# Two more slabs of each DeltaNet group as seven half-size block products, with their sums on VectorE inside the triangular inverse

## The chip, the cores and the metric

The kernel runs on one core of a Trainium2 chip, in one launch. The metric is the device time of the launch in microseconds. TensorE multiplies, VectorE and ScalarE do the elementwise work, GpSimd helps a little, and SyncE's queue issues all loads. Everything is float32.

## The reference

One transformer layer for 256 tokens of width 2048. A token mixer multiplies x by `w_in`, and its columns feed three things: an S5 branch (2048 columns, called u), a DeltaNet branch (q and k with 16 heads, v and z with 32 heads, 128 wide each), and two gates. The branches are merged and multiplied by `w_mix_out`. After a layer norm come 32 routed experts and a second layer norm. What matters here is the DeltaNet branch, cut to its core:

```python
qkv = silu(causal_depthwise_conv(qkv, conv_w))
q, k = l2_normalize(q), l2_normalize(k)
# per head and chunk: a unit lower triangular system
lower = tril(kb @ k.T * decay, -1) + eye
sol = triangular_solve(lower, [v * beta, kb * exp(g)])
# the chunks follow each other through the state S
v_new = u_chunk - w_chunk @ S
o = q_dec @ S + attn_intra @ v_new
S = S * g_last + k_dec.T @ v_new
# the output of the branch
o = o * rsqrt(mean(o * o) + eps) * norm_w * silu(z)
```

z enters only in the last line, as `silu(z)`.

## The kernel before, in words

**Stages.** A short prologue transposes x and computes the decay gates. Then come eight DeltaNet groups of four value heads and two key heads each, to about 911 us. Then the eight u slabs and the S5 scan, the output products of both branches with the gates, `w_mix_out`, and from about 1840 us on the experts, during which the loads run without a pause.

**Slabs.** A group needs six slabs of 256 columns of `w_in`, numbered r = 0 to 5: q, k, v, v, z, z. A slab is 2 MB and is loaded by SyncE's queue into `ring[r % 3]` (`load_slot`, line 347). Each load waits until the slab before it in that ring place has been used by TensorE (`bank_ready[r % 3]`).

**Slabs 0 to 3** are computed by `seven_heads` (line 689). A slab and x are each cut into 2 by 2 blocks, and the four output blocks are made of seven block products instead of eight (Strassen's scheme in Winograd's form). That is 7 x 8 = 56 products of 128 x 128 weights with 128 columns. Four of the seven need sums of blocks of x (made once, `dn_xsum`), and three need sums of blocks of the weights, which VectorE makes for each slab with four additions of 128 x 1024 numbers (`sums_one`, `sums_two`, `sums_three`, lines 1698 to 1714, into `dn_wsum[r % 2]`; one is written over the slab itself). TensorE waits for them (`prepared`) only ahead of product 16, because the first two block products use plain blocks. The seven results lie in two banks of PSUM (`dn_first`, `dn_second`), and `join_heads` (line 1770) adds them up on VectorE with five instructions.

**Slabs 4 and 5 (z)** are computed by `part` (line 668) as 32 plain products of 128 x 128 weights with 256 columns each, into bank 1 (`z0`) and bank 2 (`z1`). ScalarE takes each with one `Silu` from the bank into `zs` (lines 1434 to 1443).

Every product written in the program is two MATMUL records in the trace, so the 64 products of two z slabs are 128 records, and the 56 of another slab are 112.

**Order of a group on TensorE, written out by hand** (`group`, from line 733): the column sums for the l2 norm; slab 3; small products for the decay; `z0(0, 19)`; transposes of v; and then the inverse. Between all of these, z products serve to fill the time in which TensorE would wait for another engine.

**The inverse.** The triangular inverse runs in six levels over half blocks for both chunks c = 0, 1, and a seventh step that joins the halves. One level goes back and forth between two engines:

- TensorE forms the first products of chunk 0 and chunk 1 (line 800) and then runs `z0(19 + 2 * lv, 21 + 2 * lv)`, two z products.
- VectorE masks each result (line 1844, `Pm`).
- TensorE forms the second products of both chunks (lines 811 and 818) and then runs `z1(lv, lv + 1)`, one z product.
- VectorE subtracts them from the inverse (line 1852, called the update here). Then the next level's line 800 may run, chunk by chunk (`t_ready[c]`).

The seventh step is lines 831 and 840 with `z0(31, 32)`, `z1(8, 9)` and `z1(9, 11)` beside it.

**The chunks.** After the inverse come the products of the state (lines 849 to 874) with the remaining 21 z products of `z1` between them, each waiting for VectorE or ScalarE (`apply_dve`, `apply_act`). ScalarE squares the outputs, VectorE reduces the squares (line 1896), ScalarE takes logarithm and exponential, and VectorE scales the outputs (line 1901, `otok`). `front` (line 727) then computes slabs 0 to 2 of the next group, with `turn_outputs` (line 680), the transposes of the outputs, after slab 0. The last multiplication with `zs` is line 1910.

**SyncE's queue at the end of the groups** (line 379 on): the load of u slab 0; small loads for S5 (`lam_re`, `lam_im`, `log_dt`, four loads of `b_re` and `b_im` in runs of 64 bytes, `d_skip`); the loads of u slabs 1 and 2, which wait for `z0` and `z1` of the last group.

Of the kernel before, what the change touches and what calls it, by code (L numbers as in the profile page):

```python
# [67 lines left out]
DN_PREPARED = 1 + 4 * GROUPS  # L68
# [4 lines left out]
def build(nc, x, w_in, conv_w, a_log, dt_bias, norm_w, w_dn, lam_re, lam_im, log_dt, b_re, b_im, c_re, c_im,  # L73
# [3 lines left out]
    with ExitStack() as ctx:  # L77
# [93 lines left out]
        dn_first, dn_second = (0, 5, 1, 0), (1, 6, 2, 7)  # L171
# [173 lines left out]
        def _(sp):  # L345
# [33 lines left out]
            load_slot(S_U % RING, in_rows(w_in[:, 0:SC]), 0, U_USE)  # L379
            sp.dma_start(spar[0:NJ, 0, :], lam_re.rearrange("(j g) n -> j (g n)", g=2)).then_inc(s5_lam_loaded, 16)  # L380
# [7 lines left out]
            for r in range(1, 3):  # L388
                load_slot((S_U + r) % RING, in_rows(w_in[:, SC * r:SC * r + SC]), r, U_USE)
# [257 lines left out]
        def _(pe):  # L647
# [31 lines left out]

            def turn_outputs(g):  # L680

                pe.wait_ge(apply_dve, 4 * g + 4)
                for a in range(GV):
                    for c in range(2):
                        col = (a % 2) * T + c * P
                        last = tr(ps[3 + a // 2][:, col:col + P], otok[:, c, a], ident[:, :])
                last.then_inc(apply_pe, 1)

            def seven_heads(g, r, lo, hi):
# [3 lines left out]
                if lo == 0:  # L693
# [4 lines left out]
                    if r == 2:  # L698
                        pe.wait_ge(bank_taken[0], 2 * g + 2)
                        pe.wait_ge(bank_taken[1], 2 * g + 1)  # L700
                    if r == 3:
                        pe.wait_ge(kd_in, 1)

# [13 lines left out]
                for i in range(lo, hi):  # L717
                    if i == KD:
                        pe.wait_ge(prepared, 4 * g + 2 + r)
# [13 lines left out]
            def group(g, more):  # L733
# [26 lines left out]
                def z0(lo, hi):  # L760
                    part(16 * (2 * g + 2), 1, 1, 2 * g + 1, xT, lo, hi)

                def z1(lo, hi):
                    part(16 * (2 * g + 2), 2, 2, 2 * g + 1, xT, lo, hi)
# [5 lines left out]
                pe.wait_ge(bank_taken[2], 2 * g + 2)  # L770
                z0(0, 19)
# [19 lines left out]
                for lv in range(HALF_LEVELS):  # L791
# [11 lines left out]
                    z0(19 + 2 * lv, 21 + 2 * lv)  # L803
# [21 lines left out]
                    z1(lv, lv + 1 if whole else 8)  # L825
# [8 lines left out]
                z0(31, 2 * KD)  # L834
                z1(8, 9)
# [7 lines left out]
                z1(9, 11)  # L843
# [7 lines left out]
                z1(11, 15)  # L851
# [5 lines left out]
                for a in range(GV):  # L857
                    last = mm(ps[7][:, a * P:a * P + P], attn[:, 0, a], vn[:, 0, a], start=True, stop=True)
                last.then_inc(apply_pe, 1)
                z1(15, 18)  # L860
# [4 lines left out]
                z1(18, 24)  # L865
# [4 lines left out]
                z1(24, 28)  # L870
                pe.wait_ge(apply_dve, 4 * g + 3)
                for a in range(GV):
                    mm(ps[6][:, a * P:a * P + P], qd[:, a], Sst[:, a], start=True, stop=False)
                    last = mm(ps[6][:, a * P:a * P + P], attn[:, 1, a], vn[:, 1, a], start=False, stop=True)
                last.then_inc(apply_pe, 1)
                z1(28, 2 * KD)
# [3 lines left out]
                else:  # L880
                    part(16 * (2 * g + 3), 0, 0, 2 * g + 2, xT, 0, 4)
# [27 lines left out]
            part(16 * (2 * GROUPS + 1), 0, 0, U_USE, xT, 4, 26)  # L909
            turn_outputs(GROUPS - 1)  # L910
            part(16 * (2 * GROUPS + 1), 0, 0, U_USE, xT, 26, 2 * KD)
# [464 lines left out]
        def _(act):  # L1376
# [22 lines left out]
            with act.Fori(0, GROUPS) as g:  # L1399
# [34 lines left out]
                act.wait_ge(bank_ready[1], 2 * g + 2)  # L1434
                A(zs[:, 0:2], ps[1][:, :].rearrange("p (h t) -> p h t", h=2), ACT.Silu).then_inc(bank_taken[1], 1)
# [3 lines left out]
                A(sq[:, 0:512], ps[7][:, :], ACT.Square)  # L1439
                act.wait_ge(apply_pe, 7 * g + 6)  # L1440
                A(sq[:, 512:1024], ps[6][:, :], ACT.Square).then_inc(osq_ready, 1)
                act.wait_ge(bank_ready[2], 2 * g + 2)
                A(zs[:, 2:4], ps[2][:, :].rearrange("p (h t) -> p h t", h=2), ACT.Silu).then_inc(bank_taken[2], 1)
# [10 lines left out]
            def take_u(r):  # L1454
                act.wait_ge(bank_ready[r % 3], U_USE + r // 3 + 1)
                nc.scalar.copy(uT[:, 2 * r:2 * r + 2, :],
                               ps[r % 3][:, :].rearrange("p (k t) -> p k t", k=2)).then_inc(bank_taken[r % 3], 1)
# [220 lines left out]
        def _(dve):  # L1678
# [19 lines left out]
            def sums_one(g, r):  # L1698
# [4 lines left out]
                dve.drain()  # L1703
                V.tensor_tensor(ring[:, buf, 0:8, P:SC], ring[:, buf, 0:8, 0:P], ring[:, buf, 0:8, P:SC], ALU.subtract)

# [46 lines left out]
            def dn_group(g, more):  # L1752
# [17 lines left out]
                def join_heads(r):  # L1770

                    at_ = [4 * dn_first[r] + i for i in range(4)] + [4 * dn_second[r] + i for i in range(3)]
# [10 lines left out]
                    V.tensor_tensor(at(w0, 2, 512)[:, :, 0:P], twice(dn_partial[:, 3]), two(1, 2), ALU.add)  # L1783
# [3 lines left out]
                    V.tensor_tensor(dn_joined.rearrange("p (a n) -> p a n", a=2)[:, :, P:2 * P], twice(dn_partial[:, 2]),  # L1787
                                    two(4, 5), ALU.add)
                    V.tensor_tensor(dn_joined[:, 2 * P:3 * P], dn_partial[:, 1], regions[:, at_[3]], ALU.add)
# [3 lines left out]
                def decay(c):  # L1793

                    dve.wait_ge(gb_ready, 2 * g + c + 1)
                    for a in range(GV):
# [15 lines left out]
                                ALU.mult).then_inc(qk_ready, 1)  # L1812
                dve.wait_ge(tok_ready, 2 * g + 1)
                V.tensor_copy(ktok, ps[5][:, 0:GQ * P].rearrange("p (b d) -> p b d", b=GQ)).then_inc(tok_taken, 1)
                decay(0)
                join_heads(3)
# [24 lines left out]
                for lv in range(HALF_LEVELS):  # L1841
                    for c in range(2):
# [4 lines left out]
                                        ALU.mult).then_inc(pm_ready[c], 1)  # L1847
                    for c in range(2):
# [25 lines left out]
                def by_head(v, width):  # L1874
# [4 lines left out]
                                by_head(beta[:, 0, ds(GV * g, GV)], P), ALU.mult).then_inc(apply_dve, 1)  # L1879
                if more:  # L1880
# [13 lines left out]

                dve.wait_ge(osq_ready, g + 1)
# [4 lines left out]
                for c in range(2):  # L1900
                    V.tensor_tensor(otok[:, c], ps[7 - c][:, :].rearrange("p (a d) -> p a d", a=GV),
# [5 lines left out]
                dve.wait_ge(bank_taken[2], 2 * g + 3)  # L1907
# [556 lines left out]
```

## Time and profile before

| | us |
|---|---|
| median of 3 runs | 2832.26 (2831.66 to 2834.74) |
| the profiled execution, time | 2834.3 |
| the profiled execution, span | 2832.6 |
| TensorE busy | 2775.6 (98% of the span) |
| VectorE busy | 1252.3 (44%) |
| ScalarE busy | 446.0 (16%) |
| one group, slab 3 to slab 3 (617.04 to 728.22) | 111.18 |

Times in the trace count from the start of the span. "Idle before" stands in brackets behind a row, with what ended it. A TensorE record's duration overlaps with the next record's, so the pace of a row of products is read from start to start, not from the mean duration.

### The profile page before, as it was taken

The numbers are of one execution on the slowest core, as the hardware profiler recorded it, in microseconds if no ns is written. First come the engines' busy times: TensorE is split into PE (matmuls) and PEld (weight loads), VectorE is DVE, ScalarE is ACT, GpSimd is POOL, SyncE is SP. The second block draws the span as 40 slices with busy tenths as digits, with TensorE's granted clock in tenths as the row PEclk, the third lists the DMA queues.
The fourth block names the chain that finished last, engine by engine and source line by source line (L and its number), as shares of the span: only waits on it lengthen the run. The fifth ranks groups of instructions, "written<-read, shape, count | busy, mean of one in ns | idle before, by whom it ended". The sixth has DMA issues, their size and how long they took to land.

```text
span 2832.6 us, 53479 instructions
## 1 busy us (share of the span) xinstructions
PE 2775.6 (98%) x22343; PEld 2072.8 (73%) x22343; DVE 1252.3 (44%) x2593; ACT 446.0 (16%) x773; POOL 63.7 (2%) x115
## 2 busy tenths in 40 slices
PE   8999999999999999999999999999999999999997
PEld 8899898898898888888899999843444444444442
DVE  6566565665664327777665652221111211112114
ACT  3121121221221111110010000131112111112110
POOL 1000000000000000000000000000000000000000
PEclk9999999999999999999999999999999999999999
DMA  7233242343344523444477556378999999999997
GB/s 218 88 122 120 90 149 91 107 142 98 102 149 107 163 90 123 130 136 137 145 210 228 178 161 226 149 293 362 422 422 422 422 422 422 422 422 422 422 422 280
DMA packets 328854, 654.12 MB, mean 231 GB/s; under 512 B 45232, under 2 KB 274736, under 8 KB 279536
## 3 DMA queue, kind: packets, MB, share of 16 engines
q1 hardware_dynamic: 328688, 651.61, 62.7%
q8 instruction: 141, 2.31, 0.3%
q14 instruction: 25, 0.20, 0.0%
HBM read 649.49 MB, written 2.10 MB: 230 GB/s over the span
## 4 chain that ended last, share of the span: by engine, by line
PE 88%; DMA 7%; DVE 2%; DVEq 2%; issue 1%; ACT 0%; SPq 0%; ACTq 0%
PE bank L723 14%; PE bank L675 14%; PE bank L1054 10%; PE bank L1244 9%; PE bank L975 8%; PE bank L1282 7%; DMA arena<-in_w_up_dram 7%; PE bank L1223 4%; PE bank L1109 4%; PE bank L1322 4%; PE bank L800 1%; PE bank L818 1%; PE bank L938 1%; PE bank L811 1%; PE bank L1254 1%
## 5 line engine op out<-in xcount | busy, mean ns | idle before, releaser
L675 PE MATMUL bank<-arena 128*128 128x256 f32 x2048 | 484.8, 386 | 0.0
L1244 PE MATMUL bank<-arena 128*64 128x512 f32 x2048 | 445.5, 594 | 12.3 <-DMA arena<-in_w_up_dram 12.3
L675 PEld LDWEIGHTS bank<-arena 128*128 128x128 f32 x2048 | 374.9, 190 | 52.3
L723 PEld LDWEIGHTS bank<-arena 128*128 128x128 f32 x3584 | 403.9, 192 | 4.2 <-issue 3.8
L723 PE MATMUL bank<-arena 128*128 128x128 f32 x3584 | 405.5, 275 | 0.0
L1244 PEld LDWEIGHTS bank<-arena 128*64 128x64 f32 x2048 | 144.5, 137 | 311.3 <-issue 281.5
L1054 PEld LDWEIGHTS bank<-arena 128*128 128x128 f32 x2576 | 287.8, 192 | 0.1
L1054 PE MATMUL bank<-arena 128*128 128x128 f32 x2576 | 287.8, 275 | 0.0
L975 PE MATMUL bank<-arena 128*128 128x256 f32 x1024 | 223.5, 380 | 0.0
L2356 DVE TENSOR_SCALAR arena<-bank 128x512 f32<-128x512 f32 x16 | 11.1, 691 | 465.8 <-PE bank L1244 465.8
L975 PEld LDWEIGHTS bank<-arena 128*128 128x128 f32 x1024 | 194.0, 190 | 26.7
L1282 PE MATMUL bank<-arena 128*64 128x512 f32 x960 | 211.0, 598 | 0.5 <-ACT arena L1631 0.5
L1282 PEld LDWEIGHTS bank<-arena 128*64 128x64 f32 x960 | 67.7, 138 | 133.1 <-issue 132.4
L1621 ACT ACTIVATE arena<-bank,small 128x128 f32<-128x128 f32 x256 | 96.3, 456 | 232.0 <-PE bank L1223 232.0
L2383 DVE TENSOR_TENSOR arena<-arena,bank 128x512 f32<-128x512 f32 x120 | 82.4, 687 | 105.2 <-PE bank L1322 105.0
L1223 PEld LDWEIGHTS bank<-arena 128*128 128x128 f32 x1024 | 118.4, 196 | 12.4 <-issue 11.4
L2012 DVE TENSOR_TENSOR arena<-arena 128x256 f32<-128x256 f32 x256 | 109.3, 427 | 32.5 <-issue 15.5
L1223 PE MATMUL bank<-arena 128*128 128x128 f32 x1024 | 121.4, 281 | 0.9 <-ACTq L1577 0.9
L1109 PE MATMUL bank<-arena 128*128 128x256 f32 x512 | 114.0, 381 | 0.0
L1322 PE MATMUL bank<-arena,masks 128*128 128x512 f32 x240 | 109.8, 596 | 1.8 <-DVEq L2370 1.8
L1109 PEld LDWEIGHTS bank<-arena 128*128 128x128 f32 x512 | 96.1, 190 | 12.4
L2365 DVE TENSOR_SCALAR arena<-bank 128x512 f32<-128x512 f32 x16 | 11.1, 691 | 206.8 <-PE bank L1244 206.8
(341 smaller groups left out, 2412.8 us busy)
## 6 DMA issues: line engine op xcount, KB each, us to landing
arena<-in_w_in_dram SPq DMA_DIRECT2D x72, 2048.0 KB, 8.7
arena<-in_w_up_dram SPq DMA_DIRECT2D x64, 2048.0 KB, 16.5
arena<-in_w_gate_dram SPq DMA_DIRECT2D x64, 2048.0 KB, 13.9
arena<-in_w_down_dram SPq DMA_DIRECT2D x64, 2048.0 KB, 21.1
arena<-in_w_dn_out_dram SPq DMA_DIRECT2D x16, 2048.0 KB, 8.2
arena<-in_w_glu_b_dram SPq DMA_DIRECT2D x8, 2048.0 KB, 8.2
arena<-in_w_glu_a_dram SPq DMA_DIRECT2D x8, 2048.0 KB, 8.2
arena<-in_w_mix_out_dram SPq DMA_DIRECT2D x8, 2048.0 KB, 14.3
```

Source lines behind the costliest of these rows:

```text
L675: last = mm(ps[bank][:, ct * T:ct * T + T], ring[:, buf, k, ct * P:ct * P + P], rhs[:, k, :], start=k == 0, stop=k == KD - 1)
L723: last = mm(regions[:, 4 * bank + place % 4], left(k), right(k), start=k == 0, stop=k == KD // 2 - 1)
L975: last = mm(ps[bank][:, ct * T:ct * T + T], ring[:, n % 2, k, ct * P:ct * P + P], oT[:, half * KD + k, :], start=half == 0 and ct == 0 and ...
L1054: last = mm(banks[:, base + P * place:base + P * place + P], left(k), right(k), start=k == 0, stop=k == KD // 2 - 1)
L1109: last = mm(ps[bank][:, 0:SC], mg[:, k, m * P:m * P + P], mixw[r][:, k, :], start=k == 0, stop=k == KD - 1)
L1223: last = mm(ps[4 + b][:, k * P:k * P + P], h1[:, m, 4 * b + k], Psel[:, m].rearrange("p o c -> p (o c)"), start=m == 0, stop=m == MT - 1)
L1244: last = mm(ps[bank][CAP * o:CAP * o + CAP, :], xg[:, 4 * q + k, CAP * o:CAP * o + CAP], w[:, o, k], start=False, stop=q == 3 and k == 3, ...
L1282: last = mm(ps[4 + n][CAP * o:CAP * o + CAP, :], shT[:, k, CAP * o:CAP * o + CAP], buf[:, o, n * 512:n * 512 + 512], start=k == 0, stop=k ...
L1322: last = mm(ps[bank][:, :], pwT[:, (n // 4) * P:(n // 4) * P + P], ysb[:, (n % 4) * 512:(n % 4) * 512 + 512], start=not biased, stop=True, ...
L1621: last = A(xg[:, k, :], ps[4 + b][:, P * j:P * j + P], ACT.Identity, scale=gqk[:, k:k + 1], bias=bqk[:, k:k + 1])
L2012: V.tensor_tensor(prod, prev.unsqueeze(2).to_broadcast([P, 2, 2, NJ]), rot, ALU.mult)
L2383: V.tensor_tensor(av, av, ps[(2, 3, 0, 1)[n % 4]][:, :], ALU.add).then_inc(sc_taken, 1)
```

## The change

- Slabs 4 and 5 are computed by `seven_heads` too: 56 products with 128 columns each in place of 32 with 256 columns. Slab 4 uses banks 1 and 2, slab 5 banks 0 and 7. Slab 0 moves from banks 0 and 1 to 1 and 2.
- Their weight sums are new on VectorE: those of slab 4 around the copy of `ktok` and `decay(0)`, those of slab 5 one addition each in levels 0 to 3 of the inverse, between the two masks and the two updates.
- Their results are joined by `join_heads(4)` after the first `vn`, and `join_heads(5)` ahead of the reduction of the squares, into `zs`. ScalarE's two `Silu` read and write `zs` in SBUF and come after these joins.
- The z products are dealt out anew over the group. In level 0, four of them stand between the first products of chunk 0 and those of chunk 1.
- The outputs of the chunks go to banks 6 and 4 in place of 7 and 6. The first u slab goes to bank 5.
- At the end of the groups, u slab 1 is loaded ahead of the small S5 loads, and these wait for the end of the last `z1`; u slab 2 is loaded after them.

```diff
-DN_PREPARED = 1 + 4 * GROUPS
+DN_PREPARED = 1 + 6 * GROUPS
...
-        dn_first, dn_second = (0, 5, 1, 0), (1, 6, 2, 7)
+        dn_first, dn_second = (1, 5, 1, 0, 1, 0), (2, 6, 2, 7, 2, 7)
...
             load_slot(S_U % RING, in_rows(w_in[:, 0:SC]), 0, U_USE)
+            load_slot((S_U + 1) % RING, in_rows(w_in[:, SC:2 * SC]), 1, U_USE)
+            sp.wait_ge(bank_ready[2], U_USE)
             sp.dma_start(spar[0:NJ, 0, :], lam_re.rearrange("(j g) n -> j (g n)", g=2)).then_inc(s5_lam_loaded, 16)
             sp.dma_start(spar[0:NJ, 1, :], lam_im.rearrange("(j g) n -> j (g n)", g=2)).then_inc(s5_lam_loaded, 16)
             sp.dma_start(coef[0:NJ, 15, 0:2], log_dt.rearrange("(j g) -> j g", g=2)).then_inc(s5_lam_loaded, 16)
...
             sp.dma_start(dsk, d_skip.rearrange("(k a) q -> (a q) k", k=KD), allow_slow_non_contiguous=True).then_inc(s5_loaded, 16)
-            for r in range(1, 3):
-                load_slot((S_U + r) % RING, in_rows(w_in[:, SC * r:SC * r + SC]), r, U_USE)
+            load_slot((S_U + 2) % RING, in_rows(w_in[:, 2 * SC:3 * SC]), 2, U_USE)
...
+            def first_u(lo, hi):
+                if lo == 0:
+                    pe.wait_ge(slot_loaded[0], 16 * (2 * GROUPS + 1))
+                    pe.wait_ge(bank_taken[0], U_USE + 1)
+                for i in range(lo, hi):
+                    ct, k = divmod(i, KD)
+                    last = mm(ps[5][:, ct * T:ct * T + T], ring[:, 0, k, ct * P:ct * P + P], xT[:, k, :],
+                              start=k == 0, stop=k == KD - 1)
+                if hi == 2 * KD:
+                    last.then_inc(bank_ready[0], 1)
...
                     if r == 2:
                         pe.wait_ge(bank_taken[0], 2 * g + 2)
-                        pe.wait_ge(bank_taken[1], 2 * g + 1)
                     if r == 3:
+                        pe.wait_ge(bank_taken[2], 2 * g + 1)
                         pe.wait_ge(kd_in, 1)
+                    if r == 4:
+                        pe.wait_ge(bank_taken[2], 2 * g + 2)
+                    if r == 5:
+                        pe.wait_ge(vtok_taken, g + 1)
...
-                        pe.wait_ge(prepared, 4 * g + 2 + r)
+                        pe.wait_ge(prepared, 6 * g + 2 + r)
...
                 def z0(lo, hi):
-                    part(16 * (2 * g + 2), 1, 1, 2 * g + 1, xT, lo, hi)
+                    seven_heads(g, 4, lo, hi)
                 def z1(lo, hi):
-                    part(16 * (2 * g + 2), 2, 2, 2 * g + 1, xT, lo, hi)
+                    seven_heads(g, 5, lo, hi)
...
-                pe.wait_ge(bank_taken[2], 2 * g + 2)
-                z0(0, 19)
+                z0(0, 37)
...
-                    z0(19 + 2 * lv, 21 + 2 * lv)
+                        if lv == 0 and c == 0:
+                            z0(37, 41)
+                    if lv > 0:
+                        z0(39 + 2 * lv, 41 + 2 * lv)
...
-                    z1(lv, lv + 1 if whole else 8)
+                    z1(2 * lv, 2 * lv + 2 if whole else 16)
...
-                z0(31, 2 * KD)
-                z1(8, 9)
+                z0(51, 54)
...
-                z1(9, 11)
+                z0(54, 56)
+                z1(16, 18)
...
-                z1(11, 15)
+                z1(18, 26)
...
-                    last = mm(ps[7][:, a * P:a * P + P], attn[:, 0, a], vn[:, 0, a], start=True, stop=True)
+                    last = mm(ps[6][:, a * P:a * P + P], attn[:, 0, a], vn[:, 0, a], start=True, stop=True)
...
-                z1(15, 18)
+                z1(26, 32)
...
-                z1(18, 24)
+                z1(32, 43)
...
-                z1(24, 28)
+                z1(43, 50)
...
-                    mm(ps[6][:, a * P:a * P + P], qd[:, a], Sst[:, a], start=True, stop=False)
-                    last = mm(ps[6][:, a * P:a * P + P], attn[:, 1, a], vn[:, 1, a], start=False, stop=True)
+                    mm(ps[4][:, a * P:a * P + P], qd[:, a], Sst[:, a], start=True, stop=False)
...
-                z1(28, 2 * KD)
+                z1(50, 56)
...
-                    part(16 * (2 * g + 3), 0, 0, 2 * g + 2, xT, 0, 4)
+                    first_u(0, 4)
...
-            part(16 * (2 * GROUPS + 1), 0, 0, U_USE, xT, 4, 26)
+            first_u(4, 26)
             turn_outputs(GROUPS - 1)
-            part(16 * (2 * GROUPS + 1), 0, 0, U_USE, xT, 26, 2 * KD)
+            first_u(26, 2 * KD)
...
-                act.wait_ge(bank_ready[1], 2 * g + 2)
-                A(zs[:, 0:2], ps[1][:, :].rearrange("p (h t) -> p h t", h=2), ACT.Silu).then_inc(bank_taken[1], 1)
                 act.wait_ge(apply_pe, 7 * g + 2)
                 nc.scalar.copy(Sst, ps[4][:, :].rearrange("p (a d) -> p a d", a=GV)).then_inc(apply_act, 1)
                 act.wait_ge(apply_pe, 7 * g + 3)
-                A(sq[:, 0:512], ps[7][:, :], ACT.Square)
+                A(sq[:, 0:512], ps[6][:, :], ACT.Square)
+                act.wait_ge(bank_taken[1], 2 * g + 3)
+                A(zs[:, 0:2], zs[:, 0:2], ACT.Silu)
                 act.wait_ge(apply_pe, 7 * g + 6)
-                A(sq[:, 512:1024], ps[6][:, :], ACT.Square).then_inc(osq_ready, 1)
-                act.wait_ge(bank_ready[2], 2 * g + 2)
-                A(zs[:, 2:4], ps[2][:, :].rearrange("p (h t) -> p h t", h=2), ACT.Silu).then_inc(bank_taken[2], 1)
+                A(sq[:, 512:1024], ps[4][:, :], ACT.Square).then_inc(osq_ready, 1)
+                act.wait_ge(bank_taken[2], 2 * g + 3)
+                A(zs[:, 2:4], zs[:, 2:4], ACT.Silu)
...
-                               ps[r % 3][:, :].rearrange("p (k t) -> p k t", k=2)).then_inc(bank_taken[r % 3], 1)
+                               ps[r % 3 if r else 5][:, :].rearrange("p (k t) -> p k t", k=2)).then_inc(bank_taken[r % 3], 1)
...
-            def sums_one(g, r):
+            def sum_first(g, r):
 
                 buf = r % RING
                 dve.wait_ge(slot_loaded[buf], 16 * (2 * g + r // 3 + 1))
                 V.tensor_tensor(dn_wsum[r % 2][:, 0], ring[:, buf, 0:8, P:SC], ring[:, buf, 8:16, P:SC], ALU.add)
                 dve.drain()
+
+            def sum_own(g, r):
+                buf = r % RING
                 V.tensor_tensor(ring[:, buf, 0:8, P:SC], ring[:, buf, 0:8, 0:P], ring[:, buf, 0:8, P:SC], ALU.subtract)
+
+            def sums_one(g, r):
+                sum_first(g, r)
+                sum_own(g, r)
...
+                    to_off = w0 if r < 4 else SH + 8960 + 512 * (r - 4)
+                    to = dn_joined if r < 4 else at(to_off, 512)
+                    reach = w0 + 512 - to_off
...
-                    V.tensor_tensor(dn_joined.rearrange("p (a n) -> p a n", a=2)[:, :, P:2 * P], twice(dn_partial[:, 2]),
+                    V.tensor_tensor(to.rearrange("p (a n) -> p a n", a=2)[:, :, P:2 * P], twice(dn_partial[:, 2]),
                                     two(4, 5), ALU.add)
-                    V.tensor_tensor(dn_joined[:, 2 * P:3 * P], dn_partial[:, 1], regions[:, at_[3]], ALU.add)
+                    V.tensor_tensor(to[:, 2 * P:3 * P], dn_partial[:, 1], regions[:, at_[3]], ALU.add)
...
+                sums_one(g, 4)
+                sums_two(g, 4)
                 dve.wait_ge(tok_ready, 2 * g + 1)
                 V.tensor_copy(ktok, ps[5][:, 0:GQ * P].rearrange("p (b d) -> p b d", b=GQ)).then_inc(tok_taken, 1)
                 decay(0)
+                sums_three(g, 4)
                 join_heads(3)
...
+                    if lv == 0:
+                        sum_first(g, 5)
+                    if lv == 1:
+                        sum_own(g, 5)
+                    if lv == 2:
+                        sums_two(g, 5)
+                    if lv == 3:
+                        sums_three(g, 5)
...
+                join_heads(4)
                 if more:
                     sums_one(g + 1, 0)
...
+                join_heads(5)
...
-                    V.tensor_tensor(otok[:, c], ps[7 - c][:, :].rearrange("p (a d) -> p a d", a=GV),
+                    V.tensor_tensor(otok[:, c], ps[6 - 2 * c][:, :].rearrange("p (a d) -> p a d", a=GV),
...
-                dve.wait_ge(bank_taken[2], 2 * g + 3)
```

## Rows read from the trace of the kernel before

**Rows 1.** The page, parts 1 and 4: busy time by engine, and the chain that ended last.
```profile
PE 2775.6 (98%) x22343; PEld 2072.8 (73%) x22343; DVE 1252.3 (44%) x2593; ACT 446.0 (16%) x773; POOL 63.7 (2%) x115
...
PE 88%; DMA 7%; DVE 2%; DVEq 2%; issue 1%; ACT 0%; SPq 0%; ACTq 0%
```

**Rows 2.** Timeline of TensorE: start, us, engine, line, operation, tiles, count; one front stage.
```profile
133.88 12.67 PE L723 MATMUL bank<-arena 128*128 128x128 f32 x112
...
146.39 1.04 PE L686 MATMUL bank<-ident,arena 128*128 128x128 f32 x8
```

**Rows 3.** Timeline of TensorE, last group's end and the u slabs.
```profile
940.50 41.71 PE L675 MATMUL bank<-arena 128*128 128x256 f32 x192
982.04 3.66 PE L906 MATMUL bank<-ident,arena 128*128 128x128 f32 x32
```

**Rows 4.** Timeline of VectorE, group 0: one slab's sums and a join.
```profile
56.40 1.22 DVE L1702 TENSOR_TENSOR arena<-arena 128x1024 f32<-128x1024 f32 x1 [0.19 <-issue]
...
57.70 1.23 DVE L1704 TENSOR_TENSOR arena<-arena 128x1024 f32<-128x1024 f32 x1
...
58.84 1.22 DVE L1707 TENSOR_TENSOR arena<-arena 128x1024 f32<-128x1024 f32 x1
...
61.47 0.29 DVE L1781 COPY arena<-bank 128x128 f32<-128x128 f32 x1
...
63.78 0.61 DVE L1758 TENSOR_SCALAR arena<-arena,cw 128x256 f32<-128x256 f32 x2 [0.33 <-issue]
```

**Rows 5.** Timeline of VectorE, group 6 to 7: before and at the fourth slab's join.
```profile
734.67 1.23 DVE L1811 TENSOR_TENSOR arena<-arena 128x1024 f32<-128x1024 f32 x1 [0.19 <-issue]
...
744.20 0.29 DVE L1781 COPY arena<-bank 128x128 f32<-128x128 f32 x1 [4.12 <-PE bank L723]
```

**Rows 6.** Timeline, group 0: entry of the inverse.
```profile
87.99 0.68 DVE L1826 TENSOR_TENSOR arena<-bank,arena 128x512 f32<-128x512 f32 x1
...
88.84 0.46 PE L800 MATMUL bank<-arena 64*64 64x64 f32 x16 [1.21 <-DVEq L1830]
```

**Rows 7.** Timeline, group 0: one level of the inverse (level 3).
```profile
100.83 0.93 PE L800 MATMUL bank<-arena 64*64 64x64 f32 x32
101.36 0.88 DVE L1844 TENSOR_TENSOR arena<-bank,arena 128x256 f32<-128x256 f32 x2 [0.24 <-PE bank L800]
...
101.69 1.13 PE L675 MATMUL bank<-arena 128*128 128x256 f32 x4
...
102.75 0.46 PE L811 MATMUL bank<-arena 64*64 64x64 f32 x16
...
103.72 1.50 DVE L1852 TENSOR_TENSOR arena<-arena,bank 128x512 f32<-128x512 f32 x2 [1.48 <-PE bank L818]
...
104.29 0.70 PE L675 MATMUL bank<-arena 128*128 128x256 f32 x2
...
104.92 0.93 PE L800 MATMUL bank<-arena 64*64 64x64 f32 x32
```

**Rows 8.** Timeline, group 0: end of the inverse and the first products of the chunks.
```profile
114.89 0.65 PE L831 MATMUL bank<-arena 64*64 64x64 f32 x8 [0.19 <-DVEq L1863]
...
118.56 1.05 PE L849 MATMUL bank<-arena 128*128 128x128 f32 x8
```

**Rows 9.** Timeline, group 0: the root of the output norm on VectorE and ScalarE.
```profile
132.98 1.22 DVE L1896 TENSOR_REDUCE small<-arena 128x8 f32<-128x1024 f32 x1 [2.32 <-ACT arena L1441]
...
137.91 1.29 DVE L1901 TENSOR_TENSOR arena<-bank,small 128x512 f32<-128x512 f32 x2 [3.71 <-ACTq L1448]
```

**Rows 10.** Timeline of SyncE's queue at the end of the groups.
```profile
855.99 1.72 SPq L380 DMA_DIRECT2D arena<-in_s_lam_re_dram  x1
...
872.75 3.01 SPq L387 DMA_DIRECT2D small<-in_s_d_dram  x1
...
911.84 0.56 SPq L351 DMA_DIRECT2D arena<-in_w_in_dram  x1
```

**Rows 11.** Windows: TensorE, its loads, VectorE, ScalarE, GpSimd, clock, DMA share, GB/s.
```profile
919.00:922.00 3.00, 3.00 (x16) 2.64 (x15) 0.00 (x0) 0.00 (x0) 0.00 (x0) 1.00 0.28 85
```

More of the change, by code:

```diff
@@ L869, in group @@
                 last.then_inc(apply_pe, 1)
-                z1(24, 28)
+                z1(43, 50)
                 pe.wait_ge(apply_dve, 4 * g + 3)
                 for a in range(GV):
-                    mm(ps[6][:, a * P:a * P + P], qd[:, a], Sst[:, a], start=True, stop=False)
-                    last = mm(ps[6][:, a * P:a * P + P], attn[:, 1, a], vn[:, 1, a], start=False, stop=True)
+                    mm(ps[4][:, a * P:a * P + P], qd[:, a], Sst[:, a], start=True, stop=False)
+                    last = mm(ps[4][:, a * P:a * P + P], attn[:, 1, a], vn[:, 1, a], start=False, stop=True)
                 last.then_inc(apply_pe, 1)
-                z1(28, 2 * KD)
+                z1(50, 56)
                 if more:
@@ L1782, in join_heads @@
                     dve.drain()
-                    V.tensor_tensor(at(w0, 2, 512)[:, :, 0:P], twice(dn_partial[:, 3]), two(1, 2), ALU.add)
+                    V.tensor_tensor(at(to_off, 2, reach)[:, :, 0:P], twice(dn_partial[:, 3]), two(1, 2), ALU.add)
                     dve.drain()
```

## The prediction

> **What bounds the kernel now.** I read the page's busy times and its chain first. TensorE is busy for 98% of the span and holds 88% of the chain that ended last; VectorE is at 44% [rows 1]. So time falls only where TensorE has less to do, or waits less. The loads run without a pause only in the experts, behind everything changed here; their first loads wait for TensorE's earlier products, so what a group saves should reach the end whole.
>
> Next, the pace of the two kinds of product, from start to start. A stretch of 112 records with 128 columns takes 146.39 - 133.88 = 12.51 us, 0.1117 us a record [rows 2]. A stretch of 192 records with 256 columns takes 41.54 us, 0.2164 us a record [rows 3]. Half the columns cost 0.516 of the time.
>
> Last, the timeline of one group, since the new sums land where TensorE and VectorE hand work back and forth. Two things are to be seen there. VectorE has a pause of 1.48 us in each level, ahead of its updates [rows 7]. And at the entry TensorE already waits 1.21 us for VectorE [rows 6].
>
> **The change part by part**, for one group.
>
> *TensorE's work.* Two slabs: 128 records x 0.2164 = 27.70 us go, 224 x 0.1117 = 25.02 us come: -2.68 us. That is the gain if no wait changes. The walk below asks which do.
>
> *Entry of the inverse.* TensorE's start on chunk 1 in level 0 is set by VectorE: its work ends at 87.99 + 0.68 = 88.67, and TensorE starts at 88.84, 0.17 us later [rows 6]. That chain of VectorE begins at the join of slab 3, which waits 4.12 us for TensorE [rows 5]. The sums of slab 4 go in ahead of it. An addition followed by a drain occupies 1.30 us, one without 1.14 us [rows 4]; the first three take 1.30 + 1.14 + 1.30 = 3.74 us and the fourth 1.30. From 735.90, with about 0.5 us for the copy of `ktok` and 1.3 us for `decay(0)`, VectorE is done at about 742.8; the join starts at 744.20 [rows 5]. So they cost nothing, covered by that wait of 4.12 us, with 1.4 us to spare; without that cover they would cost 5.0 us less the pause. TensorE's own way there changes by 74 x 0.1117 - 38 x 0.2164 = +0.04 us, and the four z products before chunk 1 (0.89 us, 1.1 with the change of tile size) fit into the idle 1.21 us. Change: 0.
>
> *Levels 0 to 3.* I follow chunk 1, from its first products in one level to those in the next. Before: from 88.84 [rows 6] to 104.92 + 0.43 = 105.35 [rows 7], taking half of the pair's 0.86 for chunk 0, 16.51 us for four levels, 4.13 us each. TensorE's own path now: first products 0.86, z part 1.06 - 0.42 = 0.64 (two half-size products for two whole), second products 1.54, z part 0.65, in all 3.69 us. VectorE's path: 0.53 us from TensorE's start to the mask (100.83 to 101.36), 0.44 for the mask, 1.30 for the new addition, 0.81 to the second update, 0.69 for it, 0.17 back to TensorE [rows 4, 6, 7] = 3.94 us. It is the longer one, because the pause of 1.48 us shrinks by the 0.42 us of z work taken out, to 1.06, and the addition does not quite fit. In level 1 the addition has no drain: 3.78 us. Four levels: 3 x 3.94 + 3.78 = 15.60 us, against 16.51: -0.91 us.
>
> *Level 4 to 5*, without an addition, is TensorE's again: 4.09 to 3.71 us (0.02 of it VectorE's): -0.38 us.
>
> *Level 5 to the first product of the chunks.* The z part of level 5 is 0.42 us shorter. The step on line 831 waits for VectorE as before [rows 8], so its time from the second products stays. The next z part is six records for four, -0.20 us; the last, eight for four, +0.03 us. Together -0.59 us.
>
> *The chunks.* 42 records x 0.2164 = 9.09 us become 76 x 0.1117 = 8.49 us: -0.60 us. `join_heads(4)` occupies VectorE for 63.78 - 0.33 - 61.47 = 2.0 us, 2.1 with its end [rows 4], and then come two sums; these 4.6 us fit between the first `vn` and the next result it must take, about 5.1 us later. It is tight, and if it misses by half a microsecond TensorE has about that much left before line 868.
>
> *The output norm.* `join_heads(5)` starts at the end of z and stands ahead of the reduction, which was at 132.98 [rows 9]. It ends some 2.1 us after that, so `otok` comes at about 139.2 instead of 137.91, and the sums for slab 1 end near 145.5. `turn_outputs` comes at 146.39 [rows 2], and the sums are needed 3.6 us after it. Cost 0. Slab 1's load starts some 2 us later, with over 10 us to spare.
>
> *End of the groups.* The S5 loads now stand between the end of `z1` and u slab 2. Before, that load was issued at 911.84. The chain of small loads took 855.99 to 872.75 + 3.01 = 19.8 us of the queue, u slab 2 needs some 8.4 us more (its transfer ended at about 920.2) [rows 10, 11], so it lands at +28.2 us. TensorE wants it at 940.50 [rows 3], +28.7 us. Cost 0, bounds 0 and 6: the 0.5 us could turn into a wait if the transfers are slower, but part of the 19.8 us was waiting behind a slab's transfer which is not there now.
>
> **Sum.** -0.91 - 0.38 - 0.59 - 0.60 = -2.48 us a group, 0.2 us less than TensorE's work alone says; eight groups: -19.8 us. The profiled execution took 2834.3 us (span 2832.6), 2.0 us above the median of 2832.26. Against it: 2814.5; against the median: **2812.4 us**.
>
> **Unknown prices.** No row shows an addition inside the pause. From below: it hides wholly and TensorE's 3.69 us rules; 15.60 becomes 14.76, 6.7 us better over all groups, 2805.7. From above: each addition stands in full on the old path, 4.09 - 0.42 + 1.30 = 4.97 us a level. I take 3.94, built from rows of this very loop.
>
> **Rivals.**
>
> *A, the addition takes the place of the work saved* (slower). Place: levels 0 to 3, between masks and updates. Price at 4.97 us a level: 4 x 4.97 - 15.60 = 4.28 us a group, +34.2 us on my sum: **2846.6 us**. It decides once a level takes over 3.90 + 19.8 / 32 = 4.52 us. For it: VectorE's path is the longer one. Against: the pause is a measured wait for TensorE, and the rows leave only 0.25 us uncovered.
>
> *B, the same place at half the price*: levels of about 4.2 us, because updates and masks also slip against each other. 32 x 0.3 = 9.6 us worse: **2822 us**.
>
> *C, u slab 2 comes late* by the bound of 6 us: **2818 us**. For it: a margin of 0.5 us by old issue times.
>
> *D, half-size products are bound by their weight load.* Each record loads 128 x 128 weights whether 128 or 256 columns follow. If a load's own 0.19 us (the recorded duration on line 723) were the pace, 224 x 0.19 = 42.6 us would stand against 27.7, +15 us a group: **2950 us** and slower. 
>
> **How the numbers follow.** My forecast 0.72, A 0.03, B 0.14, C 0.08, D 0.01; the last 0.02 for a saving that ends within the noise, such as late results in the chunks. A measurement of this kernel can tell about 0.2%, 5.7 us. Faster: 0.72 + 0.14 + 0.08 = 0.94; same 0.02; slower 0.04. The range goes from 2806 (additions hidden) to 2821 (most of B, and C).
>
> **What would show it.** Right: a group lasts 108.7 us instead of 111.2; the first products of chunk 1 follow each other by 3.8 to 4.0 us in levels 0 to 3 and by 3.7 into level 5, with short idle times of TensorE on line 800's successor that end on VectorE; no idle time at slab 3's join beyond the old; L1910's place unchanged against `turn_outputs`; no wait for a load near u slab 2. Wrong: levels of 4.2 us and more (B, A), VectorE's `R` late and TensorE idle ahead of line 868, or TensorE idle for a load after u slab 1 (C).

## The result, and the profile after

The changed kernel takes 2844.85 us (median of 6 runs, 2842.1 to 2847.0), the kernel before beside it 2832.9 us: a ratio of 1.0043, 95% interval 1.0032 to 1.0055. It is slower by 12 us where 20 us less were forecast. The profiled execution has a span of 2842.8 us.

The page of the changed kernel, parts 1, 3, 4 and 5 (compare [rows 1]):

```profile
PE 2763.6 (97%) x23111; PEld 2103.9 (74%) x23111; DVE 1353.1 (48%) x2737; ACT 446.0 (16%) x773; POOL 67.1 (2%) x115
...
q14 instruction: 55, 0.45, 0.0%
...
PE 70%; DVE 13%; DMA 8%; issue 4%; DVEq 4%; ACT 0%; SPq 0%; ACTq 0%
...
L739 PE MATMUL bank<-arena 128*128 128x128 f32 x5376 | 654.1, 280 | 19.4 <-DVEq L1737 19.3
```

TensorE is busy for 12.0 us less than before, and idle for 22.2 us more (79.2 in place of 57.0 us of the span). So the work did shrink, and waits ate the gain. A part of the gain in busy time went to a lower clock besides, as experiment 1 shows. VectorE now holds 13% of the chain, where it held 2%. Line 739 is the block product of `seven_heads`, and line 1737 is where VectorE reports a slab's sums done: 19.3 us of TensorE's waits stand there, and before there were none.

The waits of TensorE in the changed kernel from 61 to 855 us (waiter, releaser, us in all, times, longest):

```profile
PE bank L739 <- DVEq L1737: 19.3, 6, 3.5
PE bank L815 <- DVEq L1902: 6.6, 23, 0.4
```

and those of VectorE in it, from 0 to 950 us:

```profile
DVE arena L1809 <- PE bank L739: 38.8, 18, 4.0
DVE arena L1809 <- issue: 38.7, 8, 6.6
```

"issue" means that VectorE waited for nothing that the profile shows. Line 1809 is the first instruction of a join, and the first that counts as busy in the group's loop. Six of the eight are 6.1 to 6.6 us long, at the six jumps back of the loop (it runs seven times; the last group is written out behind it). In the kernel before, the waits on "issue" at the starts of groups 1 to 7 were 4.6 us in all. The timeline of VectorE in the changed kernel, where it goes from group 0 to group 1:

```profile
144.73 1.41 DVE L1950 SCALAR_TENSOR_TENSOR arena<-bank,small,arena 128x512 f32 x2 [1.26 <-PE bank L698]
152.40 0.29 DVE L1809 COPY arena<-bank 128x128 f32<-128x128 f32 x1 [6.26 <-issue]
```

and of TensorE there:

```profile
144.38 16.24 PE L739 MATMUL bank<-arena 128*128 128x128 f32 x144
163.80 10.82 PE L739 MATMUL bank<-arena 128*128 128x128 f32 x80 [3.17 <-DVEq L1737]
```

The bank that the join reads had been full since the transposes began at 143.51, so the 6.26 us are no wait for data. They put slab 2's sums late, and TensorE stands for 3.17 us in slab 2, ahead of product 16. Then its clock falls, as the windows of the changed kernel behind five of its waits show (the column before the last two is the granted clock):

```profile
165.00:168.00 3.00, 3.00 (x16) 3.00 (x16) 2.24 (x8) 0.00 (x0) 0.00 (x0) 0.50 0.03 10
390.50:396.50 6.00, 5.54 (x26) 5.54 (x27) 4.80 (x13) 0.00 (x0) 0.00 (x0) 0.50 0.33 105
506.50:509.00 2.50, 2.50 (x14) 2.50 (x14) 1.83 (x7) 0.00 (x0) 0.00 (x0) 0.50 0.25 76
619.00:625.00 6.00, 5.39 (x25) 5.39 (x26) 4.80 (x13) 0.00 (x0) 0.00 (x0) 0.50 0.32 101
735.00:738.00 3.00, 3.00 (x14) 3.00 (x15) 2.36 (x7) 0.00 (x0) 0.00 (x0) 0.50 0.33 103
```

0.50 is 1.2 GHz in place of 2.4. The five spells last some 24 us together. One of the six waits (3.45 us, up to 278.94) has none behind it, and in the groups of the kernel before there is none either.

What the forecast said of the other places held, in the main. Slab 3's join still waits for TensorE, 1.47 us now, where 1.4 were to be left (compare [rows 5]). The output norm came 0.8 us later than worked out: `otok` starts 6.4 us ahead of `turn_outputs`, where it was 8.5 us before and 7.2 were forecast (compare [rows 2, 9]). That cost nothing:

```profile
75.51 0.29 DVE L1809 COPY arena<-bank 128x128 f32<-128x128 f32 x1 [1.47 <-PE bank L739]
...
133.30 1.22 DVE L1937 TENSOR_REDUCE small<-arena 128x8 f32<-128x1024 f32 x1
137.09 1.29 DVE L1942 TENSOR_TENSOR arena<-bank,small 128x512 f32<-128x512 f32 x2 [2.57 <-ACTq L1466]
...
143.51 1.04 PE L698 MATMUL bank<-ident,arena 128*128 128x128 f32 x8
```

What VectorE waits for at the jump is told by the queues. DMA queues from 172 to 839 us, the kernel before:

```profile
q8 instruction: 62, 1.02, 0.6%
q14 instruction: 1, 0.01, 0.0%
```

and the changed kernel:

```profile
q8 instruction: 65, 1.06, 0.7%
q14 instruction: 27, 0.22, 0.1%
```

q14 brings instructions in packets of 8 KB. Before, one came in six groups; now 27 come, about five a group. And about the jump from group 0 to group 1, between 145 and 160 us of the changed kernel, three of them:

```profile
q14 instruction: 3, 0.02, 0.6%
```

In the traces of the kernel before and of experiment 1 no packet of q14 falls between 145 and 160 us. And between 146.5 and 152.2 us, while VectorE stands:

```profile
q1 hardware_dynamic: 1754, 1.78, 92.2%
q14 instruction: 1, 0.01, 0.4%
```

q1 is the load of a slab. The one packet of q14 starts some 4 us after the jump, and VectorE goes on 2 us later. Whether the packet waits behind the slab's load was not tested.

VectorE's loop over the groups went from 271 to 301 instructions (drains, register and semaphore instructions counted, which the page's counts leave out). By the Trainium skill ("Runtime: NRT & Kernel Launch", section "Instruction fetch mechanics") 16 KiB hold 256 instructions; an estimate from that figure is 128 for 8 KB. The trace of experiment 2 agrees: there VectorE's loop is written out, and a packet of q14 comes for every 128 of its instructions. From this came theory F, that the start of VectorE's loop is no longer held on the chip when it jumps back, and has to be brought again. Its rival, theory O, was that VectorE simply has too much to do. It is busy for about 100 us more over the kernel.

### The profile page after: what moved, and what is told of

Same layout as the page of the kernel before. It is cut to its first block, busy times and chain, and to the rows that moved or that the text cites. A ratio compares the mean times of both kernels' runs of the same rounds, so it can differ in the third digit from the quotient of the medians.

```text
span 2842.8 us, 55264 instructions
## 1 busy us (share of the span) xinstructions
PE 2763.6 (97%) x23111; PEld 2103.9 (74%) x23111; DVE 1353.1 (48%) x2737; ACT 446.0 (16%) x773; POOL 67.1 (2%) x115
## 4 chain that ended last, share of the span: by engine, by line
PE 70%; DVE 13%; DMA 8%; issue 4%; DVEq 4%; ACT 0%; SPq 0%; ACTq 0%
PE bank L739 18%; PE bank L1072 10%; PE bank L1262 8%; DMA arena<-in_w_up_dram 8%; PE bank L1300 7%; PE bank L1241 4%; PE bank L1127 4%; DVE arena L2052 4%; PE bank L1340 4%; PE bank L676 4%; DVE arena L2054 3%; DVE arena L2056 3%; PE bank L815 1%; PE bank L1272 1%; DVE arena L1891 1%
## 5 line engine op out<-in xcount | busy, mean ns | idle before, releaser
L739 PE MATMUL bank<-arena 128*128 128x128 f32 x5376 | 654.1, 280 | 19.4 <-DVEq L1737 19.3
L739 PEld LDWEIGHTS bank<-arena 128*128 128x128 f32 x5376 | 626.0, 194 | 32.0 <-DVEq L1737 20.4
L1072 PEld LDWEIGHTS bank<-arena 128*128 128x128 f32 x2576 | 287.8, 192 | 0.1
L1072 PE MATMUL bank<-arena 128*128 128x128 f32 x2576 | 287.8, 275 | 0.0
L993 PE MATMUL bank<-arena 128*128 128x256 f32 x1024 | 223.5, 380 | 0.0
L993 PEld LDWEIGHTS bank<-arena 128*128 128x128 f32 x1024 | 194.0, 190 | 26.7
L676 PE MATMUL bank<-arena 128*128 128x256 f32 x960 | 212.1, 381 | 0.0
L676 PEld LDWEIGHTS bank<-arena 128*128 128x128 f32 x960 | 181.1, 190 | 25.0
L1241 PEld LDWEIGHTS bank<-arena 128*128 128x128 f32 x1024 | 117.4, 194 | 12.0 <-issue 11.4
L1241 PE MATMUL bank<-arena 128*128 128x128 f32 x1024 | 120.4, 279 | 0.5 <-ACTq L1595 0.5
L1127 PE MATMUL bank<-arena 128*128 128x256 f32 x512 | 114.0, 381 | 0.0
L1127 PEld LDWEIGHTS bank<-arena 128*128 128x128 f32 x512 | 96.1, 190 | 12.4
```

The source lines that it names most:

```text
L676: last = mm(ps[bank][:, ct * T:ct * T + T], ring[:, buf, k, ct * P:ct * P + P], rhs[:, k, :], start=k == 0, stop=k == KD - 1)
L739: last = mm(regions[:, 4 * bank + place % 4], left(k), right(k), start=k == 0, stop=k == KD // 2 - 1)
L993: last = mm(ps[bank][:, ct * T:ct * T + T], ring[:, n % 2, k, ct * P:ct * P + P], oT[:, half * KD + k, :], start=half == 0 and ct == 0 and ...
L1072: last = mm(banks[:, base + P * place:base + P * place + P], left(k), right(k), start=k == 0, stop=k == KD // 2 - 1)
L1127: last = mm(ps[bank][:, 0:SC], mg[:, k, m * P:m * P + P], mixw[r][:, k, :], start=k == 0, stop=k == KD - 1)
L1241: last = mm(ps[4 + b][:, k * P:k * P + P], h1[:, m, 4 * b + k], Psel[:, m].rearrange("p o c -> p (o c)"), start=m == 0, stop=m == MT - 1)
```

## The experiments

In the profiles VectorE executes 48 instructions up to the loop's start in both kernels. The experiments move that start by drains in VectorE's prologue, where it waits about 5 us for ScalarE, and touch nothing in the loop:

```diff
+            for _ in range(N):
+                dve.drain()
             dve.wait_ge(sp_done, 1)
```

**1. The changed kernel, N = 40.**

> The changed kernel with 40 drains added on VectorE in the prologue, where it waits 5 us for ScalarE; nothing in the group loop is touched. Theory F (instruction fetch): VectorE's group loop has 301 instructions in place of 271 and now runs over one more 8 KB block (128 instructions) of its instruction stream, so that the block with the loop's start is gone at each jump back; VectorE stands 6.3 us there, TensorE then waits 3.2 us at slab 2's product 16, and its clock halves. Moved 40 instructions on, the loop lies within three blocks: no stall at the jump, no wait of TensorE there, about 2813 us (2809 to 2819). Rival O (overload): VectorE has 12 us more work a group and is late whatever the place of its code: 2843 to 2849 us, with the same 19 us of TensorE's waits.

2811.78 us (2811.32 to 2817.44), ratio 0.993 (0.9916 to 0.9943) to the kernel before. Forty instructions that do nothing make the changed kernel 33 us faster. TensorE is busy for 12.3 us less than without them:

```profile
PE 2751.3 (98%) x23111; PEld 2093.0 (74%) x23111; DVE 1353.4 (48%) x2737; ACT 446.0 (16%) x773; POOL 67.0 (2%) x115
```

VectorE at the same jump in this run:

```profile
144.08 1.41 DVE L1952 SCALAR_TENSOR_TENSOR arena<-bank,small,arena 128x512 f32 x2 [1.26 <-PE bank L698]
146.22 0.29 DVE L1811 COPY arena<-bank 128x128 f32<-128x128 f32 x1 [0.72 <-issue]
```

and TensorE, whose slabs 1 and 2 now run without a break:

```profile
143.74 25.18 PE L739 MATMUL bank<-arena 128*128 128x128 f32 x224
168.75 1.88 PE L752 MATMUL bank<-arena,ones 128*128 128x512 f32 x4
```

From 172 to 819 us no packet of q14 is left, and the clock stays at 2.4 GHz through all groups. VectorE's busy time is the same 1353 us, so theory O falls.

**2. The changed kernel with VectorE's loop written out.**

```diff
-            with dve.Fori(0, GROUPS - 1) as g:
+            for g in range(GROUPS - 1):
                 dn_group(g, True)
```

> The changed kernel with VectorE's group loop written out eight times, no jump back. Theory F: same as with the 40 drains, about 2813 us (2809 to 2820); the blocks are fetched in order ahead of their use. Rival O: 2843 to 2849 us. A third reading (fetching itself is slow, jump or no jump): stalls of microseconds spread over the groups, over 2830 us.

2816.77 us (2813.06 to 2817.51), ratio 0.9941 (0.9927 to 0.9955). No stall at what was the jump: VectorE is idle for 0.2 us there. With no loop, q14 shows the instructions going by. From 218.9 to 877.8 us:

```profile
q14 instruction: 12, 0.10, 0.0%
```

From the first of these packets to the last VectorE executes 1406 instructions, 127.8 from one to the next on the average (117 to 139). So q14 does bring VectorE's instructions, 128 in a packet.

A group takes 109.18 us against 108.64 in experiment 1 (from the first column sum of group 0 to that of group 7, divided by seven). Why it is some 5 us behind in all, 4 of them in the groups, is not settled; its waits on line 815 and a few of TensorE's own ("issue", up to 1.2 us each) are a little larger.

**3 and 4. The kernel before, N = 16 and N = 40.**

> The kernel before with 16 drains added in the same place of VectorE's prologue, loop body untouched (271 instructions). Theory F: its loop ends just ahead of a block boundary (no fetch was seen in it, and the changed loop fetches at its instruction 271); pushed 16 on, it crosses, and each of seven jumps costs VectorE about 6 us and TensorE about 2 to 3: 2846 to 2860 us. Boundary guessed within 17 instructions, so there is one chance in four that 16 misses it and the time stays at 2833. Rival O: 2833 us.

> The kernel before with 40 drains there. Theory F: the loop starts in the next block and ends before a boundary again: as before, 2831 to 2835 us. If drains in the prologue cost time in themselves, it shows here as some 2 us more. Rival O: 2833 us.

2831.19 us (2829.84 to 2833.05), ratio 0.9994 (0.9985 to 1.0003), and 2832.66 us (2831.37 to 2835.28), ratio 1.0 (0.9991 to 1.001). Drains there cost nothing. The forecast for 16, a stall and 2846 to 2860 us, missed. The run placed the boundary better, since its loop starts at instruction 64 and is held.

**5. The kernel before, N = 8.**

> The kernel before with 8 drains added in VectorE's prologue (16 and 40 of them left it at 2831 to 2833 us). From the fetches seen so far, blocks of VectorE's instructions begin near its 62nd to 66th, 190th and 318th to 322nd record; the loop before is records 48 to 318. Theory F: the loop is in reach when it lies within three blocks. With 16 drains it starts at 64, in the second block. With 8 it starts at 56, in the first, and ends at 326, in the fourth: the only place where the kernel before should stall. Then 5 fetches a group on the instruction queue, a stall of VectorE of about 5.5 us at each jump, about 3 us of TensorE's wait at slab 2's product 16 and spells at half clock: 2845 to 2865 us. If it stays at 2831 to 2835, the place of the loop against the blocks does not explain it and it was something else that the 40 drains moved in the changed kernel (its length of 301 against some limit that the drains can't have changed, so theory F would be short of a part).

2879.27 us (2877.06 to 2881.3), ratio 1.0167 (1.0151 to 1.0182). Eight instructions that do nothing make the kernel before 47 us slower, while 16 or 40 do nothing to it. The direction and the place are those of the forecast; the size is 14 us over its upper end. Of these, 12 us are TensorE's waits, 5 us each where 3 were expected. VectorE and TensorE at the first jump:

```profile
155.78 0.29 DVE L1783 COPY arena<-bank 128x128 f32<-128x128 f32 x1 [6.96 <-issue]
```

```profile
167.98 12.02 PE L723 MATMUL bank<-arena 128*128 128x128 f32 x80 [5.10 <-DVEq L1712]
```

and TensorE's waits for the sums from 61 to 900 us:

```profile
PE bank L723 <- DVEq L1712: 30.1, 6, 5.1
```

In the groups 34 us pass at 1.2 GHz, and TensorE is busy for 14.9 us longer (2790.5 us against 2775.6). With the 30.1 us of waits that is 45.0 us; the profiled executions differ by 44.6 us.

**6. The price of the four additions in the pause.** From experiment 1, without them:

```diff
                     if lv == 0:
-                        sum_first(g, 5)
+                        dve.wait_ge(slot_loaded[2], 16 * (2 * g + 2))
-                    if lv == 1:
-                        sum_own(g, 5)
-                    if lv == 2:
-                        sums_two(g, 5)
                     if lv == 3:
-                        sums_three(g, 5)
+                        dve.sem_inc(prepared, 1)
```

> The changed kernel with 40 drains in the prologue (2811.8 us), without the four additions for slab 5 that stand in levels 0 to 3 (slab 5's weight sums are left out, so that z is not the reference's). It measures their price in the pause, which the prediction put at 0.84 us a group, 6.7 us in all: TensorE's path of 3.69 us then rules the levels, 2805 us. Level by level the profile with the additions shows 3.84, 3.65, 3.87, 3.86 us and about 0.9 us of waits of TensorE a group: 2804 to 2807. If the additions were hidden after all: 2811 to 2812.

4729.19 us, a time that says nothing: with another z the tokens go to other experts, and the kernel takes its branch for experts with too many tokens. The groups come before that and can be read. From the column sums of group 0 to those of group 7 they take 815.2 - 60.1 us, 107.87 us each, against 108.64 us with the additions: 0.77 us a group, 0.84 forecast.

**7. Four products moved into the waits left in the inverse.** From experiment 1:

```diff
-                    z1(2 * lv, 2 * lv + 2 if whole else 16)
+                    z1(*((0, 4), (4, 6), (6, 9), (9, 12), (12, 14), (14, 20))[lv])
```

and the bounds of all later parts of `z1` four higher, the last being `z1(54, 56)`.

> The changed kernel with 40 drains in the prologue, and four of slab 5's products moved from behind the chunks' outputs into the waits that are left in the inverse: 4, 2, 3, 3, 2, 6 of them after the second products of levels 0 to 5 in place of 2, 2, 2, 2, 2, 6. All additions stay. The waits on line 815 add up to 7.6 us in the run it is made from; if they are filled: 2805 to 2808 us. If VectorE's path gets longer by what is put in (because the masks of the next level come later): 2811 to 2813 us.

2808.56 us (2804.4 to 2813.1), ratio 0.9919 (0.9905 to 0.9933). Its waits on line 815 in the groups:

```profile
PE bank L815 <- DVEq L1904: 2.7, 8, 0.3
```

down from 7.6 us. A group takes 107.70 us, 0.94 less than in experiment 1, where the waits had been 0.95. The median lies half a microsecond above the range that was expected. The two medians differ by 3 us with spreads of 6 and 9, so the gain shows in the groups' length more than in the total. This version has the lowest median of all that were run.

**8 and 9. The changed kernel, N = 16 and N = 112.**

> The changed kernel with 16 drains in place of 40. Theory F with the blocks as the runs so far place them (beginning near VectorE's record 62 to 64, 190, 318, 446): the loop of 301 records starts at 64 and ends at 364, three blocks: 2811 to 2815 us. If the first block ended later than at 64, the stall stays: 2843 to 2848 us.

> The changed kernel with 112 drains. By the same blocks the loop starts at record 160, in the second block, and ends at 460, in the fifth: it touches four blocks again, so the stall comes back although nothing was taken away: 2844 to 2852 us, of which up to 3 us are the drains themselves, that no longer all fit into VectorE's wait of 5 us. If any shift that is long enough helps: 2812 to 2816 us.

2814.73 us (2813.03 to 2816.62), ratio 0.9937 (0.9921 to 0.9954), and 2850.59 us (2848.92 to 2851.86), ratio 1.0065 (1.0048 to 1.0082). So it is no matter of enough drains: with more of them the stall is back, and TensorE's waits for the sums are 22.9 us. The waits of VectorE in the run with 112, from 61 to 900 us:

```profile
DVE arena L1811 <- issue: 40.0, 7, 6.8
```

Experiment 8 has no stall at the jump, and is 3 us above experiment 1. Its group 0 holds a wait of TensorE of 1.4 us that ended on "issue", with a spell at 1.2 GHz behind it; where that wait comes from was not looked into.

The eight kernels with these two loops, by the place of VectorE's loop in its instructions:

| kernel, drains | loop from, to | us | stall at the jump |
|---|---|---|---|
| before, 0 | 48, 318 | 2832.9 | no |
| before, 8 | 56, 326 | 2879.3 | yes |
| before, 16 | 64, 334 | 2831.2 | no |
| before, 40 | 88, 358 | 2832.7 | no |
| changed, 0 | 48, 348 | 2844.9 | yes |
| changed, 16 | 64, 364 | 2814.7 | no |
| changed, 40 | 88, 388 | 2811.8 | no |
| changed, 112 | 160, 460 | 2850.6 | yes |

With blocks of 128 instructions that begin near 63, 191, 319 and 447, the rule is the same in all eight: no stall where the loop touches three blocks, an idle time of 6.1 to 7.0 us at the jump, in place of 0.6 to 0.8, where it touches four. Experiments 6 and 7, with loops from 88 too, are held as well. The block's length is shown by experiment 2's packets. Where the blocks begin, and that three of them stay in reach, is read from these eight: a profile shows when a packet comes, not what is held.

## Why the prediction was wrong

**The step that failed** is the one that is not there. The walk gave each added instruction of VectorE the time it executes and a place to hide it, and took for granted that the loop round them runs as before. It goes from "Entry of the inverse" to "The output norm", which ends with the sums for slab 1. Between that and the next group lie VectorE's jump back and the sums for slab 2, and the walk has no term for them: it put them at nothing without a reason. There VectorE's work moved by 5.5 us (6.26 less the 0.72 of experiment 1), at each of six jumps, through 30 instructions that carried the loop's end from instruction 318 to 348, over a boundary at about 319. TensorE had 2.4 us to spare there and waits for the rest: 19.3 us in six groups. About 24 us at half clock follow, and TensorE is busy for 12.3 us longer than in experiment 1. Together that is 31.6 us, and the profiled executions of the two differ by 32.2 us.

The kernel before stood within a few instructions of this: its loop ends at 318, and 8 more in front of it cost 47 us. Nothing in its busy times, waits or chain tells so. What did tell was q14 on the page of the kernel before:

```profile
q14 instruction: 25, 0.20, 0.0%
```

That is 25 packets for the whole kernel, thus a loop that is held; I did not count what would become of it.

The Trainium skill ("Runtime: NRT & Kernel Launch", section "Instruction fetch mechanics") says: instructions are brought ahead in order, and a jump back to a page that is no longer in the window costs a fetch. The runs agree in kind. It gives pages of 16 KiB and a window of two. Here VectorE's packets are of 8 KB, and by the table three blocks of 128 instructions stay in reach.

**What held, read from experiment 1**, where the stall is away. The time: 2811.8 us against 2812.4 forecast. A group: (820.71 - 60.25) / 7 = 108.64 us, against (839.38 - 60.90) / 7 = 111.21 before: -2.57 us where -2.48 was worked out. That the time fits within a microsecond is in part luck, since misses of opposite sign cancel in it: in group 0 the four levels gave 0.4 us more than worked out, and the step to level 5 gave 0.1 us less.

*The levels.* TensorE's first products in experiment 1, chunk 1 of level 0, both chunks of level 1, then level 2 and a part of level 4:

```profile
88.06 0.46 PE L815 MATMUL bank<-arena 64*64 64x64 f32 x16
...
91.09 0.46 PE L815 MATMUL bank<-arena 64*64 64x64 f32 x16 [0.37 <-DVEq L1904]
...
91.90 0.46 PE L815 MATMUL bank<-arena 64*64 64x64 f32 x16 [0.35 <-DVEq L1904]
...
95.12 0.92 PE L815 MATMUL bank<-arena 64*64 64x64 f32 x32
...
103.28 0.63 PE L815 MATMUL bank<-arena 64*64 64x64 f32 x16 [0.19 <-DVEq L1904]
```

From 88.06 to 91.90 it is 3.84 us, and from 88.06 to 103.28, four levels, 15.22 us. I had 3.94 and 15.60. VectorE's path is the longer one, as forecast, only 0.1 us shorter than the sum of its parts: its addition starts right behind the mask. Level 4 to 5 took 3.84 us instead of 3.71.

*The rivals.* A (the additions cost what was saved) did not come: levels of 3.8 us, not 4.5, and experiment 6 puts the additions at 0.77 us a group. The sign came out as in A, for another reason. B would be levels of 4.2 us: no. C: the S5 loads in the changed kernel,

```profile
924.66 0.51 SPq L382 DMA_DIRECT2D arena<-in_s_lam_re_dram  x1
...
940.32 1.08 SPq L351 DMA_DIRECT2D arena<-in_w_in_dram  x1
```

take 15.7 us of the queue ahead of u slab 2 instead of 19.8 (perhaps because no slab is on its way ahead of them; that was not tested), and TensorE starts u slab 2 at 953.39 with no wait. D (half-size products bound by their weight load) did not come either: 224 records in 25.01 us from 143.74 to 168.75 are 0.1117 us each, as before.

## What to carry to other kernels

Before you add work to an engine that runs in a hardware loop, count the loop's instructions (drains and semaphores too) and look at the instruction queue of the page: few packets mean a loop that is held, and a few instructions more, even in front of it, can end that (here from 25 packets to 55). If a first instruction of a loop waits on "issue" for microseconds and instruction packets come in every round, move the loop or write it out, before judging the change by its time. A short wait of TensorE can then cost more than itself: behind 17 of the 18 waits of 3 to 5 us in the changed kernel and in experiments 5 and 9 the clock fell.

## What the runs showed of the hardware that was not expected

- VectorE's instructions come in packets of 8 KB, one for every 128 of them, as experiment 2 shows.
- The place of a loop matters, not only its length. The same 271 instructions took 2832.9, 2879.3, 2831.2 and 2832.7 us with 0, 8, 16 and 40 drains in front, and the same 301 took 2844.9, 2814.7, 2811.8 and 2850.6 us with 0, 16, 40 and 112.
- A jump back that is missed leaves VectorE idle for 6.1 to 7.0 us instead of 0.6 to 0.8, with two to four packets of q14 in the 15 us behind it.
- The changed kernel has six waits of TensorE of 3.0 to 3.5 us in the middle of steady products. Behind five of them it ran at 1.2 GHz, some 24 us in all, and that cost 12.3 us. In experiment 5 each of the six waits, of 5.0 to 5.1 us, had such a spell behind it. The forecast had no term for that.
